# Expert routing done tile by tile inside the recurrence, with token rows scattered to per-expert regions in DRAM

## The reference, cut to what matters

```
x = x + gt1 * (concat([y_r, y_g]) @ w_out)
h = rmsnorm(x) * (1 + sc2) + sh2
lg = h @ w_router_group + b          # 4 groups, the best one is taken
le = h @ w_router_expert + b         # its 4 experts, the best two are taken
wts = pg_top * top_v / sum(top_v)
out = sum over the two experts e of wts[e] * ((silu(h @ gate[e]) * (h @ up[e])) @ down[e])
y = rmsnorm(x + gt2 * out) * (1 + scf) + shf
```

## Time and profile before

| | us |
|---|---|
| median of 3 runs | 1575.67 (1574.25 to 1575.81) |
| the profiled execution, its own time | 1577.13 |
| span of the profiled execution | 1575.4 |
| PE busy in the span | 1446.2 (92%) |
| DVE busy | 526.7 (33%) |
| ACT busy | 371.3 (24%) |
| POOL busy | 184.1 (12%) |
| the lowest slice of PE (of 40), from about 1063 to 1102 us | 4 tenths |

### The profile page before, as it was taken

How to read it: one execution, slowest core, us unless ns; L and a number is a source line. 1 busy time by engine, 2 the same in 40 slices (tenths; PEclk the granted TensorE clock), 3 DMA queues, 4 the chain that set the end, 5 groups by cost and what they waited for, 6 DMA issues and landing times. The chain is left out here.

```text
span 1575.4 us, 28583 instructions
## 1 busy us (share of the span) xinstructions
PE 1446.2 (92%) x12005; PEld 1042.5 (66%) x12005; DVE 526.7 (33%) x988; ACT 371.3 (24%) x766; POOL 184.1 (12%) x303
## 2 busy tenths in 40 slices
PE   5799999999996899999999999964999999999965
PEld 3466666566664877777777777634887878788831
DVE  4244644530211454544544544346000010000017
ACT  5231331311212323224223223120101111111122
POOL 1002112110001212102102102001000000000043
PEclk9899999999998999999999999985999999999988
DMA  8337566441233621321321311026969997888457
GB/s 319 112 98 238 175 201 227 161 145 60 78 102 134 220 58 52 109 52 59 108 60 51 108 36 41 1 60 226 341 229 378 380 392 295 311 327 327 158 206 262
DMA packets 167856, 271.70 MB, mean 172 GB/s; under 512 B 18336, under 2 KB 88862, under 8 KB 167728
## 3 DMA queue, kind: packets, MB, share of 16 engines
q1 hardware_dynamic: 153504, 222.47, 42.0%
q0 software_dynamic: 11920, 38.99, 6.5%
q10 hardware_dynamic: 2304, 8.39, 1.3%
HBM read 215.22 MB, written 54.59 MB: 171 GB/s over the span
## 5 line engine op out<-in xcount | busy, mean ns | idle before, releaser
L2162 PEld LDWEIGHTS banks<-moe_xT,moe_wg 128*128 128x128 f32 x1024 | 131.3, 191 | 8.9 <-issue 7.8
L2162 PE MATMUL banks<-moe_xT,moe_wg 128*128 128x128 f32 (+4 forms) x1024 | 135.3, 290 | 0.8 <-ACT moe_xT L2265 0.8
L2162 PE MATMUL banks<-moe_xT,moe_wu 128*128 128x128 f32 (+4 forms) x1024 | 134.5, 290 | 0.9 <-DMA moe_wu<-w_expert_up 0.9
L2162 PEld LDWEIGHTS banks<-moe_xT,moe_wu 128*128 128x128 f32 x1024 | 131.2, 191 | 1.1 <-DMA moe_wu<-w_expert_up 1.1
L1548 POOL TENSOR_TENSOR mixer_LTm<-mixer_LT,level 128x256 f32<-128x256 f32 (+1 forms) x90 | 72.0, 822 | 401.7 <-ACT mixer_LTo L1605 276.2
L653 PE MATMUL banks<-xT,w_v 128*128 128x352 f32 (+1 forms) x384 | 118.7, 469 | 0.0
L653 PE MATMUL banks<-xT,w_r 128*128 128x352 f32 (+1 forms) x384 | 118.6, 469 | 0.0
L653 PE MATMUL banks<-xT,w_k 128*128 128x352 f32 (+1 forms) x384 | 118.3, 468 | 0.0
L1275 PE MATMUL banks<-mixer_w_out,mixer_yT 128*128 128x512 f32 x256 | 115.3, 607 | 0.0
L2191 PE MATMUL banks<-moe_wd,moe_hid 128*128 128x512 f32 x256 | 112.5, 592 | 0.0
L653 PEld LDWEIGHTS banks<-xT,w_v 128*128 128x128 f32 x384 | 72.6, 190 | 45.2 <-issue 2.2
(11 more groups left out here) (457 smaller groups left out, 1944.3 us busy)
## 6 DMA issues: line engine op xcount, KB each, us to landing
moe_wg<-w_expert_gate SPq DMA_DIRECT2D x16, 2048.0 KB, 9.4
moe_wu<-w_expert_up SPq DMA_DIRECT2D x16, 2048.0 KB
moe_wd<-w_expert_down SPq DMA_DIRECT2D x16, 2048.0 KB, 11.3
feats<-w_ada SPq DMA_DIRECT2D x8, 2048.0 KB
wada<-w_ada SPq DMA_DIRECT2D x4, 2048.0 KB
feats<-w_ada_final SPq DMA_DIRECT2D x4, 2048.0 KB
expert_rows<-moe_yrow ACTq DMA_DIRECT2D x16, 512.0 KB, 6.2
expert_rows<-moe_xTo SPq DMA_DIRECT2D x16, 512.0 KB
```

What stands on the lines that cost most here:

```text
L2162: mm = pe.matmul(bank[:, i * n:(i + 1) * n], wt[:, p % 2, q, (t0 + i) * P:(t0 + i + 1) * P], xT[:, p % 2, q, 0:n], start=q == 0, stop=q == ...
```

## The change

Region: a new DRAM tensor `xs` ("expert_inputs") holds 1152 rows for each of the 16 experts. A token's row is written to row (expert x 1152 + its rank among that expert's tokens), so that the rank alone, which depends only on tokens before it, says where it goes.

- In the recurrence, in step n from 2 to 7, DVE routes tile n-2 (`route`, 15 instructions) between `update(5)` and `add(0)`, PE ranks it (`rank`, two products of 16 columns between `wo0b` and `wo1a`, one for tile 0), DVE turns ranks into rows (`ranks`, 6 instructions) between `add(0)` and `add(1)`, and POOL scatters h2 with two indirect DMAs. `norm` now waits for the scatter of the tile that h2 held, in place of its store; SP stores h2 for the last two tiles only. Tile 6 is routed at the end of the block, tile 7 just before the last logits.
- The first 192 rows of each region are written with zeros first: POOL clears x1, and SP issues 32 DMAs from it after the features of tile 1. DVE's `constants()` waits for all of them.
- In the experts block DVE routes tile 8, the ranks and rows of tiles 7 and 8 are made, and POOL scatters both from xg, into which SP has loaded them. After `order` SP loads the first gate matrix, waits for the four scatters, loads the rows of the first two tiles itself with three plain DMAs whose address comes from `order`, waits for them, and then loads the up and down matrices. The one-hot tables, the plan and the gathers by it are gone; what was done before them for the slots is done later, beside PE's products (`sizes`, `rows`, `shares`, `blocks`). POOL's `take` for later tiles uses plain DMAs, and POOL writes zeros behind the last token of each region before extra passes could read there.

The core of the diff:

```diff
             load_x(0, P)
             constants()
             load_feats(1, 1, P)
+
+            sp.wait_ge(sg("x1_zeroed"), 1)
+            for e in range(NE):
+                for lo, hi in ((0, P), (P, S_MAX)):
+                    sp.dma_start(d["xs"][e * CAP + lo:e * CAP + hi, :], x1[0:hi - lo, :]).then_inc(sg("xs_zeroed"), 16)
...
                 dve.wait_ge(sg("rows_made"), 2)
                 dve.wait_ge(sg("router_loaded"), 64)
+                dve.wait_ge(sg("xs_zeroed"), 32 * NE)
...
+                        if name == "wo1a" and n >= 2:
+                            rank(n - 2, 6 * n + 6)
...
+                if n >= 2:
+                    pool.wait_ge(sg("xs_zeroed"), 32 * NE)
+                    pool.wait_ge(sg("rows_found"), n - 1)
+                    pool.wait_ge(sg("h2_made"), n - 1)
+                    for i in range(2):
+                        pool.indirect_dma_start(out=d["xs"], out_offset=bass.IndirectOffsetOnAxis(ap=c["row"][:, n - 2, i:i + 1], axis=0),
+                                                in_=h2[:, :], in_offset=None).then_inc(sg("h2_scattered"), 16)
...
-                    w(dve, "h2_stored", 16 * (n - 1) + 1)
+                    if n <= NP:
+                        w(dve, "h2_scattered", 32 * (n - 1))
+                    else:
+                        w(dve, "h2_stored", 17)
...
                 if not first and m_next:
+                    if n >= 2:
+                        route(V, then, c, n - 2, sg("either_made"))
                     add(0)
+                    if n >= 2:
+                        ranks(n - 2)
                     add(1)
                     norm()
...
+            def first_tokens():
+
+                sp.wait_ge(sg("lanes_made"), 1)
+                sp.wait_ge(sg("h2_scattered"), 64)
+                for i in range(2):
+                    kind, at = TILES[i]
+                    for p in range(NE):
+                        n, lane, lo = (tail_of(p), TAIL_AT[p] - at * P, S_MAIN) if kind == "tail" else (P if p == at else 0, 0, 0)
+                        if n and 0 <= lane < P:
+                            r = sp.value_load(order[0:1, p:p + 1], min_val=0, max_val=NE - 1) * CAP
+                            sp.dma_start(xg[lane:lane + n, i, :], d["xs"][bass.ds(r + lo, n), :]).then_inc(sg(f"first{i}_loaded"), 16)
+                for i in range(2):
+                    arrived(sp, i)
...
                 sp.dma_start(wg[:, u], gate[:, bass.ds(e, 1)].rearrange("p e k n -> p (e k) n")).then_inc(sg(f"gate{u}_loaded"), 16)
+                if first:
+                    first_tokens()
                 w(sp, "up_done", before)
```

More of the change, by code:

```diff
@@ L119, in build @@
             "by_place": sb("by_place", [P, 2, NE]),
+            "earlier": sb("earlier", [P, 4, 4]),
+            "first_row": sb("first_row", [P, NE]),
+            "group": sb("group", [P, NT, NG]),
+            "le": sb("le", [P, NT, EG]),
+            "place4": sb("place4", [P, NT, EG]),
+            "either": sb("either", [P, NT, NE]),
+            "chosen": sb("chosen", [P, NT, 2, NE]),
+            "rank": sb("rank", [P, NT, NE]),
+            "taken_so_far": sb("taken_so_far", [P, NE]),
+            "route": [sb(n, [P, 4, 4]) for n in ("ahead", "beats", "tmp16")],
+            "four": [sb(n, [P, 4]) for n in ("place_g", "top2", "picked")],
+            "slot16": sb("slot16", [P, NE]),
+            "slot32": sb("slot32", [P, 2, NE]),
+            "row_f": sb("row_f", [P, 2]),
+            "row": sb("row", [P, NT, 2], I32),
         }
@@ L1979, in experts_block, with loads_of, loaded, arrived @@
             TILES.append(("main", p_))
+        def loads_of(i):
+            kind, at = TILES[i]
+            return 1 if kind == "main" else len([p_ for p_ in range(NE) if tail_of(p_) and TAIL_AT[p_] // P == at])
+        def loaded(i):
+            return 16 * sum(loads_of(j) for j in range(i % 2 + 2, i + 1, 2)) if i >= 2 else 16 * loads_of(i)
+        def arrived(eng, i):
+            eng.wait_ge(sg(f"x{i % 2}_loaded" if i >= 2 else f"first{i}_loaded"), loaded(i))
         def tail_tile(g):
@@ new lines, in shares @@
+            def shares():
+                for i in range(2):
+                    then(V.tensor_scalar(picked[i][:, :, :], place4[:, :, :], float(i), None, ALU.is_equal))
+                dve.wait_ge(sg("ex_made"), 1)
+                then(reduce(pg[:, :], ex[:, :, :], ALU.add))
+                dve.wait_ge(sg("ex_made"), 2)
+                then(reduce(emax[:, :], prob[:, :, :], ALU.add))
+                for v in (pg, emax):
+                    then(V.reciprocal(v[:, :], v[:, :]))
+                then(V.tensor_tensor(prob[:, :, :], prob[:, :, :], wide(emax[:, :], E4), ALU.mult))
+                for i, v in enumerate((v1, v2)):
+                    then(V.tensor_tensor(taken4[:, :, :], prob[:, :, :], picked[i][:, :, :], ALU.mult))
+                    then(reduce(v[:, :], taken4[:, :, :], ALU.add))
+                then(V.tensor_tensor(emax[:, :], v1[:, :], v2[:, :], ALU.add))
+                then(V.reciprocal(emax[:, :], emax[:, :]))
+                then(V.tensor_tensor(pg[:, :], pg[:, :], emax[:, :], ALU.mult))
+                for i, v in enumerate((v1, v2)):
+                    then(V.tensor_tensor(share[:, :, i], pg[:, :], v[:, :], ALU.mult))
@@ L2526, in over_pass @@
                     V.tensor_copy(hoT[:, u, :, :], psum[4][:, 0:256].rearrange("p (a b) -> p a b", a=2)).then_inc(sg("hoT_made"), 1)
+            sizes()
             put_tail(0)
             put_main(0)
+            rows()
             for p in range(NE):
                 expert(p)
+                if p == 0:
+                    shares()
+                if p == 1:
+                    blocks()
                 if p == 6:
```

345 lines of the change are left out of this document (189 added, 156 removed).

## The result

The changed kernel takes **1597.49 us** (median of 4 runs, 1595.56 to 1598.15) against 1575.74 for the kernel before in the same session (1574.25 to 1578.33): ratio **1.0137**, 95% interval 1.0113 to 1.0161. It is 21.7 us slower. The forecast was 1577.2 with a range of 1571 to 1585; the measured time lies above that range. The profiled execution has a span of 1596.3 us, 20.9 more than before.

The account below looks back on a forecast made before the run. The passage from last logits to first expert product was taken as bounded by a chain of waits. Terms -14.7 + 11.7 + 1.5 + 3.1 = +1.6 us gave 1577.2 us on the median of 1575.67, range 1571 to 1585.

Parts of the forecast that it names:

- The wait for the zeros: DVE in `constants()`: 12.6 MB at 414 GB/s take 30.4 us, landing at 572.7; PE's next product +11.7 us.
- the clock behind it: PE at the low clock level after the wait for the zeros: +1.5 us (0 to 2).
- the passage: Last logits to first expert product: rebuilt chain puts the first gate product at 1083.7 instead of 1098.44, -14.7 us.
- The ranks: Recurrence: 13 products of 16 columns, two passes each, in PE's stream: +3.1 us (2 to 5).
- Rival D: Zero writes alone are slower, 350 GB/s: they last 36 us, +5.6, total 1582.8; chance 0.08.
- the lower bound of 44 us and a loss of 25: Zero writes at 284 GB/s, the rate of a fully busy stretch of small pieces; the forecast stayed with 414.
- Rival B: Passage: first rows 4 us late, gate load and scatters sharing engines; saving 10 instead of 14.7, total 1582; chance 0.16.
- The up matrix: Experts' start: asked for at 1080.2, lands at 1088, PE wants it at 1089; fits by 1 us.
- signs that would prove me wrong: Included PE waiting for the up matrix (moe_wu), and the clock of the first expert products below 1.
- What hides: Recurrence: DVE's routing and `ranks` fit its idle time; `norm`'s new scatter wait taken as nothing, bounds 0 to 2 us a step.
- rival A: Recurrence: scatter lands after 8 us instead of 5.5, `norm` late in six steps: +9 us, 1586; chance 0.14.
- rival C: `constants()`: zeros written by 561 don't hold DVE, needing 630 GB/s; total 1564; chance 0.04.

Follow-up runs that it names:

- e6: Changed kernel with the same 12.6 MB of zeros written as 48 DMAs of 64 rows, all from the lower 64 partitions: 1620.18 us, one run.
- e11_mid_rows: Changed kernel with the sixteen 64-row zero DMAs reading partitions 32 to 95 instead of 0 to 63: 1589.68 us, ratio 1.0068 to before.
- e2: Changed kernel with the 64-row zero DMAs made 128 rows too, 16.8 MB instead of 12.6: 1595.22 us, one run.
- e8: e1 with SP issuing the first token loads before the gate matrix, without waiting for their arrival: 1580.70 us, ratio 0.9999 to before.
- e12: e7 with the 64-row zero DMAs reading partitions 32 to 95: 1577.40 us, ratio 0.9997 to before.
- e10: e1 with the two 16-column rank products done twice in each step from tile 1 on: 1595.69 us, one run.
- e1: Changed kernel with DVE's wait for the zeros moved from `constants()` to just before the first `add(0)` in step 1: 1574.33 us, ratio 1.0006 to before.
- e4: Changed kernel with ACT's queue issuing the first token loads, up and down matrices asked for right behind the gate matrix: 1592.69 us, ratio 1.0139 to before.
- e7: Changed kernel with the edits of e1 and e4 together: 1576.13 us, ratio 0.9969 to before.

## Why the prediction was wrong

Two terms of the sum failed, and by about as much. The sum gave +1.6 us and the spans differ by 20.9, which is 19.3 more. The wait for the zeros is 8.8 of it (+20.5 for +11.7) and the clock behind it 1.3; the passage is 10.2 (-4.5 for -14.7). The ranks are right to 0.2; low clock elsewhere adds 2.8, and the start, the experts and the combine block take 3.6 away. Either of the two terms alone would have put the time just beyond the range (1577.2 + 10.1 = 1587.3, or + 10.2 = 1587.4); both together gave 1597.49.

**The zeros: the first step that failed.** "At that rate 12.6 MB take 30.4 us, and the last write lands about 1 us later: 572.7." The bytes, the start near 541.3, the place of the wait and who stands behind it were all right. The rate was not: the row of 414 GB/s in the earlier trace rows is a stretch of zero writes of 512 KB, each from all 128 partitions, and I priced sixteen DMAs of 64 rows by it. Such DMAs run at 212 (e6). DVE's update started at 580.66. e11_mid_rows is the forecast's kernel in this respect: with both halves of SBUF in each DMA the update starts at 573.82, 1.1 us from the number. The trap stood in the diff ahead of the prediction, `x1[0:hi - lo, :]`, where `hi - lo` is 64 for every other DMA. The one rule of the Trainium skill that I weighed, the HBM side at 358 GB/s (DMA: Bandwidth & Descriptors, Where 436 GB/s comes from), would have given a loss of 16.5 us, nearer to what came, but for a wrong reason here: e2 and e11 write 416 and 415 GB/s. Rival D had the right sign and too small a size (36 us of writes, 1582.8), and its "half way between the two rows" had no mechanism behind it; the lower bound of 44 us and a loss of 25 took the real value in, but I did not carry it into the range.

**From the zeros to PE, and the clock.** +11.7 us was the product's delay with zeros at 572.7; the same reading in the changed kernel gives 19.9, which is the missing 8 us of writing. That I read it at PE's product and not at DVE's update (22.05 late) was right: PE had 2.2 us of other work between the two. For the clock behind the wait I took 1.5, "0 to 2"; it was 2.8 behind 15.4 us of idle PE. In e11_mid_rows, behind 7.2 us of idle PE, the product stands at 574.21, 13.0 late, and the first addition at 604.50, 14.75 late, so the clock took 1.7. That kernel is 10.7 us slower than before (6.5 to 15 by its interval). With the rate as forecast, both terms are close to the forecast; that it is still some 10 us slower, and not level with before, is about what the passage (below) falls short by. Up to the last logits there are 2.8 us more at the low clock, for which I had nothing: a step is 1.56 us longer when the low level falls into it (60.63 us at a mean clock of 0.97 instead of 59.07 at 1.00), and this happened three times in the changed profile and twice in the one before; the rest lies behind the last full step. In the profiles of the other kernels, which have the same recurrence there, none (e11) to four (e8, e12) of these six steps are hit, so I hold this for scatter of the profiles and not for a cost of the change.

**Ranks.** Predicted +3.1, "2 to 5". Measured 0.23 for tile 0 and 0.45 for each of tiles 1 to 4; the same for tiles 5 and 6, whose products lie in a stretch with other low clock and can't be read singly, makes 2.9. Right, and e10 shows that it is the passes.

**The passage: the second step that failed.** Predicted -14.7 at the first gate product; measured -9.5. Up to SP's first token load the rebuilt chain holds to 1.4 us: with 28.4 us added for the later start, `order` was expected at 1097.1 and came at 1097.84, the gate load 1098.1 and 1099.32, the last scatter 1097.0 and 1098.41. What failed is the arrival: turns forecast at 1107.5, measured 1112.60. I counted 5.1 us for the gate matrix and 5.5 for a scatter as if each had the engines alone. The windows of the changed kernel:

```profile
1098.00:1103.00 5.00, 0.00 (x0) 0.00 (x0) 4.07 (x20) 0.47 (x2) 1.96 (x3) 0.50 0.89 234
1103.00:1108.00 5.00, 0.00 (x0) 0.00 (x0) 0.00 (x0) 0.00 (x0) 0.00 (x0) 0.50 1.05 372
1108.00:1112.00 4.00, 0.00 (x0) 0.00 (x0) 0.00 (x0) 0.00 (x0) 0.00 (x0) 0.50 0.92 199
```

Beside the scatters everything moves at 234 GB/s, and the last four microseconds, in which the rows arrive, run at 199. Two of the three row loads are 64 and 48 rows within one half of xg, the same trap as the zeros; that this has a part in it was not tried by itself. Neither this nor the reading of rows just scattered is slow by itself: e8 has the same three loads, and with the engines free PE turns the rows 1.5 us after the last issue. Rival B named this case and its number, a saving of 10, and had 0.16.

**The up matrix.** "It fits by 1 us." It was asked for 5.1 us later than forecast (1113.71 instead of 1108.6) and landed 12.2 us after, not 7.8; POOL's four loads for the next tile had gone in between. PE waited 3.11 us and then ran 7.15 us for 5.4 at a partly low clock (0.60 from 1126 to 1129, 0.83 to 1132), so that of 9.5 us saved 4.5 were left. I had listed both as signs that would prove me wrong, and priced neither. A chain with 1 us to spare, behind a transfer that is uncertain by 4 (the 4 us of rival B), can be a wait; the sum should have held it.

**What hides** was right: `norm` waits for ACT as before (1.78 us) in the six steps, and no step is longer than the ranks and the clock make it, so rival A (0.14) didn't come. Once, for tile 7 behind the scatter of tile 6, `norm` waits 4.04 us for POOL's DMA, until 1068.66. I had listed such a wait as a sign of being wrong, but it costs nothing: PE works through its output projection until 1076.5 meanwhile and turns h2 without a gap. Routing and `ranks` on DVE are free.

e1 shows the second failure in the whole time, without the first. With no wait for the zeros the forecast's terms give -11.6 us, the 1564 of rival C; e1 is at +0.9 (-2.7 to +4.4). That its ranks and its passage nearly cancel is a coincidence of sizes and was not forecast.

## What to carry to other kernels

Before a rate from the profile is used for another transfer, look at which partitions both touch: here 64 rows that lie in one half of SBUF took as long as 128 (212 against 415 GB/s), so place them across the middle. A wait for a bulk transfer belongs directly in front of the instruction that needs it; here the same wait two places later cost nothing, and at its first place everything. When a passage is bounded by several transfers, count the bytes that must land before each product and all queues that share the engines; here a change of the order alone only moved the wait (e8).

## What the runs showed of the hardware that was not expected

- Writes from SBUF to DRAM run at 407 to 416 GB/s when each DMA covers both halves of SBUF, at 212 with 64 rows in the lower half; the DMA share reads 1.02 to 1.03 in the one and 0.97 to 0.98 in the other, so the share hardly shows it, and the GB/s column does.
- DMAs from partitions 32 to 95 run at the full rate (408 to 415 GB/s in a mixture in which half of the DMAs are of this kind); from partitions 0 to 63 and 64 to 127 in turns they don't (306 to 331 GB/s in the same mixture).
- Rows just scattered are turned 1.5 us after the last issue of their loads with the engines free (e8), and 5.8 to 6.3 us after it with one to three 2 MB loads under way, whichever queue issues them (SP in the changed kernel and e1, ACT in e4 and e7).
- A step of the recurrence takes 1.56 us more when the granted clock falls in it (mean 0.97 instead of 1.00), and how many of six steps are hit differs, from none to four, between profiles of kernels that are the same there.
